# A chunked recurrence on one core: the next chunk's key, value and Gram work moved between the levels of the triangular solve

## What is computed

```python
def rwkv_scan(s0, r, decay, k, v, kk, a):
    def step(s, inp):
        r_t, w_t, k_t, v_t, kk_t, a_t = inp
        sa = jnp.einsum('bhij,bhj->bhi', s, -kk_t)
        s = s * w_t[:, :, None, :] + sa[..., None] * (kk_t * a_t)[:, :, None, :] + v_t[..., None] * k_t[:, :, None, :]
        return s, jnp.einsum('bhij,bhj->bhi', s, r_t)
```

## Time and profile before

| | us |
|---|---|
| three runs | 1494.76, 1498.63, 1498.16 |
| median | 1498.16 |
| profiled execution | 1490.45 |
| its span | 1488.8 |
| stretch of the recurrence with its fills, up to the sample state products (L1438) | about 250 |

### The profile page before, as it was taken

One profiled execution on the slowest core, in us unless ns is written; L12 is line 12 of the kernel. 1 busy time (PEld: TensorE's weight loads), 2 busy tenths in 40 slices (PEclk: granted clock), 3 DMA queues, 4 the chain that ended last, 5 costly groups with the idle time before them and its releaser, 6 DMA issues.

```text
span 1488.8 us, 30697 instructions
## 1 busy us (share of the span) xinstructions
PE 1460.0 (98%) x12466; PEld 1140.7 (77%) x12466; DVE 845.7 (57%) x1703; ACT 414.2 (28%) x900; POOL 189.2 (13%) x256
## 2 busy tenths in 40 slices
PE   9999999999999999999999989999999999999997
PEld 8887578777777776886667758888788888888886
DVE  7655058633343346415776346676666666666664
ACT  3112362123233215116776541102211110110101
POOL 1000324432122213204000410000000000000000
PEclk9999999999999999999999999999999999999999
DMA  6222543211111238447100975332222222222221
GB/s 260 86 85 71 181 161 125 79 47 49 42 47 45 88 123 257 165 132 219 45 2 2 289 275 225 135 99 85 71 85 86 85 83 75 84 85 86 97 87 60
DMA packets 57400, 163.96 MB, mean 110 GB/s; under 512 B 7312, under 2 KB 19696, under 8 KB 55952
## 3 DMA queue, kind: packets, MB, share of 16 engines
q1 hardware_dynamic: 48608, 121.46, 24.7%
q0 software_dynamic: 7936, 39.40, 7.6%
q10 hardware_dynamic: 720, 1.16, 0.2%
HBM read 144.01 MB, written 22.15 MB: 112 GB/s over the span
## 4 chain that ended last, share of the span: by engine, by line
PE 95%; DVE 3%; issue 1%; ACT 1%; DMA 0%; SPq 0%; DVEq 0%; ACTq 0%
PE acc L1040 26%; PE acc L1187 14%; PE acc L1953 5%; PE acc L1981 5%; PE acc L1962 5%; PE acc L1212 5%; PE acc L2006 3%; PE acc L1707 2%; PE acc L1731 2%; PE acc L1135 2%; PE acc L1323 2%; PE acc L1720 2%; PE acc L1150 2%; PE acc L1340 1%; PE acc L1052 1%; PE acc L1075 1%
## 5 line engine op out<-in xcount | busy, mean ns | idle before, releaser
L1040 PE MATMUL acc<-sb_work,sb_ring 128*128 128x272 f32 x602 | 150.9, 393 | 0.0
L2488 ACT ACTIVATE sb_omemT<-acc 128x272 f32<-128x272 f32 x74 | 29.3, 396 | 386.0 <-PE acc L1953 234.2
L1040 PE MATMUL acc<-sb_work 128*128 128x272 f32 x530 | 133.1, 393 | 0.0
L1040 PEld LDWEIGHTS acc<-sb_work,sb_ring 128*128 128x128 f32 x602 | 114.7, 190 | 23.3
L1040 PEld LDWEIGHTS acc<-sb_work 128*128 128x128 f32 x530 | 100.8, 190 | 21.2 <-issue 0.8
L1187 PE MATMUL acc<-sb_work,sb_ring 128*128 128x272 f32 x360 | 100.8, 409 | 0.6 <-DVE sb_work L2691 0.6
L1953 PE MATMUL acc<-sb_work,sb_ring 128*128 128x272 f32 x308 | 77.2, 393 | 1.0 <-issue 1.0
L1212 PE MATMUL acc<-sb_work,sb_ring 128*128 128x272 f32 x320 | 77.7, 396 | 0.0
L1962 PE MATMUL acc<-sb_work,sb_ring 128*128 128x272 f32 x308 | 77.1, 393 | 0.0
L1187 PEld LDWEIGHTS acc<-sb_work,sb_ring 128*128 128x128 f32 x360 | 63.8, 190 | 14.7 <-issue 1.7
L1212 PEld LDWEIGHTS acc<-sb_work,sb_ring 128*128 128x128 f32 x320 | 59.8, 190 | 14.7 <-issue 3.3
(11 more groups left out here) (488 smaller groups left out, 2805.8 us busy)
## 6 DMA issues: line engine op xcount, KB each, us to landing
sb_ring<-w_stream SPq DMA_DIRECT2D x144, 512.0 KB, 3.5
sb_work<-pages SPq DMA_DIRECT2D x56, 192.0 KB, 4.2
branch_gates<-sb_work SPq DMA_DIRECT2D x24, 272.0 KB, 2.5
sb_work<-branch_gates POOLq DMA_DIRECT2D x8, 816.0 KB, 15.0
sb_ring<-w_stream SPq DMA_DIRECT2D x16, 384.0 KB, 3.5
sb_work<-mem_kT SPq DMA_DIRECT2D x8, 512.0 KB, 8.1
sb_work<-mem_v SPq DMA_DIRECT2D x8, 512.0 KB, 10.7
query_features<-sb_work SPq DMA_DIRECT2D x10, 272.0 KB, 3.8
```

The source lines that it names most:

```text
L1040: mm = pe.matmul(out, w[:, q, :], x[q], start=q == 0, stop=q == n - 1)
```

## The change

The order is rewritten on TensorE, ScalarE and VectorE, and with it the table of fill steps and the places where GpSimd makes weight sums. Chunk 0's b, k, v and Gram work runs in a preamble. In the loop, chunk c+1's `turn_bk` stands between `solve_y` and `solve_x` of level 1, its two Gram products in the same place of levels 2 and 3, its `turn_v` on level 4. They all use `acc[2]` now, which brings new waits for the copies out of it. The prompt chunks' fills stand at five places of 3, 3, 5, 5 and 5 steps (21) where there were fourteen of 1 to 3 (22); the preamble has 12 steps, and the places 0 to 6 of the short chunk have 10 where they had 14. All in all there are as many steps as before.

```diff
         for c in range(NCH):
-            for r, n in {0: 1, 2: 2, 3: 3, 4: 2, 5: 1, 6: 2, 7: 1, 8: 2, 9: 1, 10: 2, 11: 1, 12: 2, 13: 1, 14: 1}.items():
+            for r, n in {4: 3, 6: 3, 8: 5, 10: 5, 12: 5}.items():
                 plan((c, r), n)
-        for r, n in {0: 2, 2: 2, 3: 4, 4: 2, 6: 4, 12: 8, 7: 8, 8: 4, 9: 3, 10: 1}.items():
+        for r, n in {4: 4, 6: 6, 12: 8, 7: 8, 8: 4, 9: 3, 10: 1}.items():
...
             def turn_bk(c, n):
                 pe.wait_ge(staged, c + 1)
+                if c == 1:
+                    pe.wait_ge(v_rows, 1)
+                elif c:
+                    pe.wait_ge(yt_out, c - 1)
+                else:
+                    pe.wait_ge(bo_out, PAIRS)
...
             def out_w(c, t0):
-                pe.wait_ge(bk_rows, c + 2)
+                pe.wait_ge(v_rows, c + 2)
...
             for c in range(NCH + 1):
-                n, t0, levels = (C, c * C, 5) if c < NCH else (TS, TP, 1)
-                turn_bk(c, n)
-                fill((c, 0))
-                grams(c, n, t0, 0)
+                n, t0, levels = chunk(c)
                 if c:
                     out_w(c - 1, t0 - C)
-                fill((c, 1))
-                grams(c, n, t0, 1)
-                fill((c, 2))
-                turn_v(c, n)
+                solve_first(c, n)
+                fill((c, 4))
                 if c:
                     out_u(c - 1, C)
-                fill((c, 3))
-                solve_first(c, n)
-                fill((c, 4))
-                for l in range(levels):
+                solve_y(c, n, 0)
+                if c:
+                    out_s(c - 1)
+                solve_x(c, n, 0, levels == 1)
+                fill((c, 6))
+                for l in range(1, levels):
+                    after, t1, _ = chunk(c + 1)
                     solve_y(c, n, l)
-                    if c and l == 0:
-                        out_s(c - 1)
-                    fill((c, 5 + 2 * l))
+                    if l == 1:
+                        turn_bk(c + 1, after)
+                    elif l == 4:
+                        turn_v(c + 1, after)
+                    else:
+                        grams(c + 1, after, t1, l - 2)
                     solve_x(c, n, l, l == levels - 1)
-                    fill((c, 6 + 2 * l))
+                    if l < levels - 1:
+                        fill((c, 6 + 2 * l))
```

More of the change, by code:

```diff
@@ L897, in _ @@
                 stage(c, c * C, C)
[L899 removed]
+            while summed < N_SEVEN and 28 * summed - 12 <= sums_ahead(NCH):
                 fill_sums(summed)
@@ L2248, in y_copy, with bk_copy @@
                                halves(acc[2][:], C)[:, :, :, 0:n], ACT.Copy).then_inc(yt_out, 1)
-            for c in range(NCH + 1):
-                n, t0, levels = (C, c * C, 5) if c < NCH else (TS, TP, 1)
+            def bk_copy(c, n):
                 act.wait_ge(tb_mm, c + 1)
```

108 lines of the change are left out of this document (70 added, 38 removed).

## The result

Over 14 runs each, the changed kernel took 1486.49 us (median) and the kernel before 1493.99 us; the ratio is 0.9944 with a 95% interval of 0.9927 to 0.9961. On 1494 us that is 8.4 us less, between 5.8 and 10.9. The forecast took 12.5 us off 1498.16 us. That the median came out 0.8 us from the forecast is partly luck: the median of before was itself 4 us lower when more runs stood behind it. The test of the working is the difference: 12.5 us lies above the measured interval, so the gain was smaller than predicted.

A forecast was written before the change was run, and what follows sets the result against it. TensorE's issued work bounds the kernel, 98% busy. Preamble 9.2, chunk 0 24.0, chunks 1 to 7 192.5, short chunk 10.8, stall 0.6: 237.1 against 249.6 us, so 1498.16 - 12.5 = 1485.7 us, range 1480 to 1491.5.

The forecast's parts named there:

- The chunk period: Prompt chunk on TensorE: small groups 16.72 us, five fills 10.6, `out_w` wait 0.2; 27.5 us in place of 29.39.
- `out_w`'s wait of 0.2 us: End of each chunk: ScalarE's copy of `turn_v` is ready 1.05 us after the last `solve_x` starts, which fills 0.85.
- no wait of level 4's masks: VectorE masks behind `gram_half` and `x_first`: 0.1 to 0.5 us to spare; rival of late masks 4.8 us back, chance 0.14.
- the bare wait of chunk 0: Level 0 of chunk 0, nothing between `solve_y` and `solve_x`: a 0.8 us wait for the mask.
- The price of 0.2 us for a run: Every run of fill steps, whatever its length, costs about 0.2 us for one switch, beside 0.458 us a step.
- The short chunk: Last chunk of the recurrence, half-size groups and ten fill steps: 10.8 us, with a range of half a microsecond.
- the prediction's signs of being wrong: Level 4's `solve_x` over 1.62 us after its `solve_y`, small groups over 0.87 us apart, or a longer stretch after L1438.
- A third, a longer tail: Sign of being wrong: the stretch after L1438, behind the recurrence, takes longer than before; it was forecast untouched in its order.
- The step that failed: the preamble: TensorE's groups ahead of chunk 0 summed to 9.2 us, the last four-step fill run at 2.03, with no wait.
- A rule applied in one place only: VectorE's `x_first` contending with GpSimd's SBUF reads, weighed at level 4: a possible 0.6 us wait, taken as none.
- I allowed 0.6 us for one: Term added to the recurrence's 236.5 us for one stall of the unexplained kind, giving 237.1.
- The slower rival of the prediction: Instruction supply stalls TensorE among small matmuls: 16 stalls cost 12.8 us, three a chunk 19.2, giving 1505; chance 0.04.

The follow-up runs named there:

- the split: Changed kernel with the five-step fill runs split into runs of one and four; chunk period 28.01 us, 0.40 more; ratio to before 0.9966.
- experiment 7: Changed kernel with preamble join before `x_first` and values' transposes before level 4's `solve_y`: 1481.35 us; also with the new plan 1481.22; instead with later weight load 1480.71.
- the new plan: Third edit of experiment 7: three of chunk 0's fill steps moved, two to the preamble's last run, one before level 0's `solve_x`; 1481.22 us, ratio 0.9905.
- experiment 5: Changed kernel with GpSimd's 1.5 MB load of the initial states issued behind the last fill-weight sums; chunk 7's `solve_y` 0.84 us instead of 1.74, later `out_w` part 2.67.

## Why the prediction was right, and where it was not

**Right by its steps.** The chunk period: 27.5 us predicted, 27.61 measured. Inside it the fill runs (1.57 for three steps, 2.49 for five), `out_w`'s wait of 0.2 us, no wait of level 4's masks, `out_s` on time in the prompt chunks, and the bare wait of chunk 0 (0.77 us for 0.8) are as written. The price of 0.2 us for a run is one of the switch from large to small matmuls, as the split showed: a run behind transposes adds none. The short chunk took 10.94 us for 10.8. Two of the prediction's signs of being wrong came up by the letter: `solve_x` of level 4 starts 1.65 us behind its `solve_y` (the sign was 1.62), and `solve_y` of level 0 is 0.92 us from the next group (0.87). Both are hundredths of a microsecond in a sum that missed a chunk by 0.11. A third, a longer tail, came up in the first pair of traces and not in the second.

**The step that failed: the preamble.** The forecast time came out, but the gain in the stretch was put 5.6 us too high, and the time fits because the median of before fell by 4 us meanwhile, which is luck. The sum walked PE's groups in the preamble, 9.2 us with the last fill run at 2.03 us, and gave it no wait. It took 11.73 us (289.35 to 301.08). I had checked `x_first`'s new place against level 4's masks, but the change also leaves `x_first` of chunk 0 in the preamble ahead of `join_fill((0, 2))`, and PE's next fill run now comes sooner than it did. The price is 2.3 us of wait, plus 1.6 us where the granted clock falls behind it. Moving the one join took this wait away and left one of 0.92 us for `x_first`: that shows the cause, and that 1.6 us of the 2.3 were the join's place in the queue. The rest is `x_first` being late itself.

**A rule applied in one place only.** `x_first` was slow there because GpSimd worked beside it: L2813 took 2.24 us for two with the sum of 1.27 us (L845) beside its start, and 1.12 in chunk 2; L2816 took 1.52 beside the staging copies, and 1.12. The prediction had these prices from the earlier trace rows and weighed them for level 4 alone, where it rightly took none. The Trainium skill (SBUF — State Buffer, "Who interferes with whom") says that only the port pair that VectorE and GpSimd share makes them contend; the trace agrees in the preamble, and for chunks 1 to 7 of the changed kernel the operations take 1.12 us a pair throughout. No run separates this slowness from the join's place.

**The stalls.** I allowed 0.6 us for one; three came, 2.1 us in all, in both traces of the changed kernel, about what the kernel before has (1.9 us). The slower rival of the prediction, instruction supply, if that is what they are, thus exists at a sixth of the size that it needed: it decides nothing here. In experiment 7 the stalls were 1.5 us larger with the new plan, as much as the plan had won, but they differ by 0.9 us there without a change of order too.

**The remainder.** Chunk 7 was taken as 27.5 us like the others; with the short chunk's small Gram products in its gaps it takes 26.36 where nothing stalls (the run with the delayed load of experiment 5). Preamble and chunk 0: +4.5 us, chunks 1 to 7: +1.1, short chunk: +0.1 against the sum; together the 5.7 us by which 242.75 exceeds 237.1. In the undisturbed second trace it is 4.0. Where the gain lies shows in the same pieces: against before, that trace has 6.9 us more up to the first `out_w`, 13.1 less in chunks 1 to 7 and 2.4 less in the short chunk. Nothing changed behind the recurrence, as predicted; the difference of 3 us in the first pair of traces was one execution's wait against another's.

## What to carry to other kernels

When an order is rewritten, walk the queue of every helper engine at the seams (preamble, first and last pass) as closely as in the steady loop: the steady loop was predicted to 0.1 us a chunk, and a queue in the preamble, looked at less closely, cost 2.3 us of wait, of which one moved line gave 1.6 back, and 1.6 more where the clock fell. Long runs of like-shaped matmuls are worth 0.2 us for each switch to small ones that they save here, and a gap whose halves are masked one after the other costs 0.2 us bare, so measure a gap before covering it. Once the tensor engine is full, the next microseconds lie in rare waits: a store that lands late beside big loads, and the lower clock that can follow. And single traces of such a kernel differ by a microsecond or more in one stretch, so a gain of that size needs more than one.

## What the runs showed of the hardware that I had not expected

- A wait of 2.3 us in an otherwise full TensorE was followed by a fall of the granted clock to its lower level (0.56 and 0.59 over the next 4 us in the first trace) in five of eight traces, and not in the other three. In the tail, waits of 3.3, 3.5, 4.4 and 5.2 us were each followed by one of 0.50, those of 2.7 us and less by none. The clock's price was 1.6 us in the preamble and 2.4 to 3.9 us in the tail, of the order of the wait itself.
- Packets of 16 KB of instructions stand among the data in the profile of the DMA engines. At the end of a load of 1.5 MB TensorE lost 0.9 us, and 1.8 us where the load had been moved to, each time 2.4 us behind such a packet, with no semaphore to show for it; the profile calls it "issue".
- A store of 272 KB took 2.0 us on quiet queues, 13.7 and 17.6 us (medians) while 2 MB and more were being loaded, and 7.4 us with 2 MB of these loads issued later.
